# Group norm of the last RWKV chunk in two column ranges, its channel groups inside the projection's steps, and the inverse's updates on all four quarters of TensorE

## What is computed

```python
def _rwkv7_step(S, inp):
    r, w, k, v, a, b = inp
    sa = jnp.einsum('bhij,bhj->bhi', S, a)
    S = S * w[:, :, None, :] + sa[..., None] * b[:, :, None, :] + v[..., None] * k[:, :, None, :]
    return S, jnp.einsum('bhij,bhj->bhi', S, r)
...
    mu = o.mean(-1, keepdims=True)
    var = jnp.square(o - mu).mean(-1, keepdims=True)
    o = ((o - mu) * lax.rsqrt(var + LNX_EPS)).reshape(B, T, D) * lnx[0] + lnx[1]
    o = o + (jnp.sum(rh * kh * r_k, -1, keepdims=True) * vh).reshape(B, T, D)
    out = (o.astype(x.dtype) * g) @ w_out
```

## Time and profile before

| | us |
|---|---|
| median of 3 runs | 1201.16 |
| the profiled execution's own time | 1203.65 |
| its span, first to last instruction | 1201.9 |
| TensorE's granted clock over the span | 0.949 of full speed |
| from the end of the sixth chunk's levels to the projection's first matmul, by the trace | 47.5 |

### The profile page before, as it was taken

One profiled execution on the slowest core, in us unless ns is written; L12 is line 12 of the kernel. 1 busy time (PEld: TensorE's weight loads), 2 busy tenths in 40 slices (PEclk: granted clock), 3 DMA queues, 4 the chain that ended last, 5 costly groups with the idle time before them and its releaser, 6 DMA issues.

```text
span 1201.9 us, 23503 instructions
## 1 busy us (share of the span) xinstructions
PE 1075.0 (89%) x10193; PEld 755.6 (63%) x10194; DVE 537.5 (45%) x1052; ACT 358.0 (30%) x720; POOL 70.2 (6%) x101
## 2 busy tenths in 40 slices
PE   4989988899978969999999799998878599999994
PEld 3977987899955654445553499976646544444542
DVE  5856535656457561222122654485433731212215
ACT  3435524443322431111110534463232511111102
POOL 2002000011000000000000111021100000000000
PEclk8989979999987979999999999999988899999998
DMA  9503020011031939999999902454752489999992
GB/s 332 209 23 70 1 66 3 3 38 38 26 120 65 361 144 408 423 423 423 423 423 404 385 12 92 165 216 148 270 209 68 184 338 422 422 423 423 422 412 84
DMA packets 58251, 274.16 MB, mean 228 GB/s; under 512 B 5169, under 2 KB 5690, under 8 KB 34082
## 3 DMA queue, kind: packets, MB, share of 16 engines
q1 hardware_dynamic: 48160, 237.58, 49.2%
q0 software_dynamic: 9360, 34.72, 9.0%
q10 hardware_dynamic: 626, 0.32, 0.1%
HBM read 266.18 MB, written 6.46 MB: 227 GB/s over the span
## 4 chain that ended last, share of the span: by engine, by line
PE 75%; DVE 11%; DMA 6%; ACT 3%; issue 2%; DVEq 1%; SPq 0%; POOLq 0%; ACTq 0%; POOL 0%
PE ps L742 69%; DMA arena<-in_moe_w_up 5%; ACT arena L1492 2%; PE ps L883 1%; PE ps L1381 1%; DVE arena L1932 1%; DMA arena<-in_cache_k 1%; ACT arena L1495 1%; DVE arena L2195 1%; PE ps L1089 1%; PE ps L1206 1%; DVE pwr_lo L1938 0%; DMA arena<-in_x_prompt 0%; DVE arena L2032 0%; PE ps L1254 0%
## 5 line engine op out<-in xcount | busy, mean ns | idle before, releaser
L742 PE MATMUL ps<-arena 64*64 64x64 f32 (+10 forms) x7348 | 621.4, 321 | 51.7 <-DVE arena L2382 10.8
L742 PEld LDWEIGHTS ps<-arena 64*64 64x64 f32 (+4 forms) x7348 | 353.6, 140 | 295.7 <-issue 215.2
L1495 ACT COPY arena<-ps 128x512 f32<-128x512 f32 (+7 forms) x294 | 121.5, 433 | 330.8 <-PE ps L742 182.2
L2277 DVE TENSOR_TENSOR arena<-arena,ps 128x512 f32<-128x512 f32 x16 | 17.3, 1084 | 164.2 <-PE ps L742 164.2
L1492 ACT ACTIVATE arena<-ps,arena 128x256 f32<-128x256 f32 (+5 forms) x96 | 45.6, 508 | 125.1 <-PE ps L742 94.5
L2288 DVE SCALAR_TENSOR_TENSOR yy_lo<-ps,arena,yy_hi 128x512 fp32r<-128x512 f32 x32 | 22.7, 747 | 123.1 <-ACT yy_hi L1492 123.1
L1492 ACT ACTIVATE pw_hi<-arena 128x1024 fp32r<-128x1024 f32 x40 | 42.0, 1057 | 89.5 <-PE ps L742 83.1
L742 PE MATMUL ps<-px_hi,pw_hi 128*128 128x336 f32 x192 | 62.7, 326 | 3.1 <-DVE px_lo L2165 1.8
L742 PE MATMUL ps<-px_lo,pw_hi 128*128 128x336 f32 x192 | 60.9, 317 | 0.0
L742 PE MATMUL ps<-px_hi,pw_lo 128*128 128x336 f32 x192 | 60.7, 316 | 0.0
L1492 ACT ACTIVATE yy_hi<-ps,arena 128x512 fp32r<-128x512 f32 x32 | 20.5, 684 | 106.3 <-PE ps L742 106.3
(11 more groups left out here) (227 smaller groups left out, 1386.4 us busy)
## 6 DMA issues: line engine op xcount, KB each, us to landing
arena<-in_moe_w_gate SPq DMA_DIRECT2D x64, 1024.0 KB, 15.4
arena<-in_moe_w_up SPq DMA_DIRECT2D x64, 1024.0 KB, 18.6
arena<-in_moe_w_down SPq DMA_DIRECT2D x64, 1024.0 KB, 16.8
arena<-in_rwkv_w_rkv SPq DMA_DIRECT2D x6, 2048.0 KB, 19.4
arena<-in_w_kv_shared SPq DMA_DIRECT2D x4, 2048.0 KB, 19.7
arena<-in_cache_k POOLq DMA_DIRECT2D x16, 512.0 KB, 4.6
arena<-in_cache_v POOLq DMA_DIRECT2D x16, 512.0 KB, 6.6
arena<-in_rwkv_w_out SPq DMA_DIRECT2D x2, 2048.0 KB, 10.5
```

Source lines behind the costliest of these rows:

```text
L742: return pe.matmul(out, lhsT, rhs, start=start, stop=stop)
L1495: return act.copy(out, in_)
L2277: tt(HH.rearrange("p (k q) -> p q k", k=NF), HS.rearrange("p (q k) -> p q k", k=NF), bank(3).rearrange("p (q k) -> p q k", k=NF), ALU.mult ...
```

## The change

One matrix L is also written with its two heads exchanged, so that XI of a head lies on the other head's partitions; Y is made off the diagonal, the XI update on the diagonal and the XU update off it, into two banks that alternate. The last chunk's norm is split into columns 0 to 255 (earlier chunks, means before the last solution) and 256 to 335; variances go to 32 rows of each quarter of partitions, and so does the reciprocal; bonus sums and gates are pulled ahead and put into SBUF by ACT; the rest of each channel group's scaling follows inside the projection's steps. The state's output goes after the projection's sixth step. `w_out` is loaded by rows into slots 4 and 0.

```diff
+            return {5: 0, L_WO: 4, L_WO + 1: 0}.get(n, n % NSLOT)
...
+        def sums_bank(lv, hf):
+            return (0, 2)[(lv + 1) % 2] + hf
+        def products_bank(lv, hf):
+            return 2 * ((lv + hf) % 2)
...
-            sp.wait_ge(S("out_wkvp"), 32)
+            for h in range(2):
+                if h == 0:
+                    sp.wait_ge(S("wkvs_mm"), after("wkvs_mm", 8))
+                else:
+                    sp.wait_ge(S("st_mm"), NCH - 1)
...
+                        if layer == 0 and i == 2:
+                            sp.wait_ge(S("pw_lo"), 4)
+                        if layer == 0 and i == 3:
+                            sp.wait_ge(S("wkvp_mm"), after("wkvp_mm", 1))
...
+            pool.wait_ge(S("z_ready"), after("z_ready", 8))
+            gains(0, 0)
+            ld(mconst, cd[:, mconst0:mconst0 + nM], "in_mconst")
...
             pool.wait_ge(S("wkvp_ready"), after("wkvp_ready", 1))
             for hp in range(2):
                 pool.dma_start(O["new_wkv_prompt"][0, 0].rearrange("(c e) i j -> e i c j", e=2)[hp],
                                QW[:, :, 64 * hp:64 * hp + 64]).then_inc(S("out_wkvp"), 16)
...
                 for c in range(NC):
-                    for q in QH:
-                        m = mm(ps[q, 0, 64 * c:64 * c + 64], rav[q, c, 64:128], BK[q, c, 0:64])
+                    for hp, q in enumerate(QH):
+                        mm(ps[q, 0, 64 * c:64 * c + 64], rav[q, c, 64:128], BK[q, c, 0:64])
+                    for hp, q in enumerate(QH):
+                        m = mm(ps[QH[1 - hp], 2, 64 * c:64 * c + 64], rav[q, c, 64:128], BK[q, c, 0:64])
...
-                                m = mm(ps[q, hf, 64 * (c % 4):64 * (c % 4) + 64], LM[q, c, :], XU[k % 2][q, c, :])
+                                m = mm(ps[QH[1 - hp], sums_bank(lv, hf), 64 * (c % 4):64 * (c % 4) + 64], LM[q, c, :], XU[k % 2][q, c, :])
...
+                        b = products_bank(lv, hf)
+                        for c in range(4 * hf, 4 * hf + 4):
+                            cols = slice(64 * (c % 4), 64 * (c % 4) + 64)
+                            if lv < LEVELS[k] - 1:
                                 for q in QH:
+                                    mm(ps[q, b, cols], YI[q, c, :], XI[q, c, :])
+                            for hp, q in enumerate(QH):
+                                m = mm(ps[QH[1 - hp], b + 1, cols], XI[q, c, :], YI[q, c, :])
...
+            gate(0, 0, "g_mm")
+            gate(1, 2, "g_mm")
             right_sides(NCH - 1)
+            early_means(0, 1)
+            early_means(1, 3)
             solve(NCH - 1)
+            for i in range(2):
+                early_means(2 + i, 2 * i)
+            for i in range(2):
+                bonus(i, 1 + 2 * i, "bn_mm")
             outcome(NCH - 1)
+            for c in range(NC):
+                m = variances(c, slice(0, 256))
+            for j, b in enumerate((4, 7)):
+                for c in range(4):
+                    m = mm(ps[:, b, 80 * c:80 * c + 80], bones, T3[:, 4 * j + c, 256:T])
+            for i in range(2):
+                bonus(2 + i, 2 * i, "bt_mm")
+            for i in range(2):
+                bonus(4 + i, 1 + 2 * i, "bt_mm")
+            for c in range(NC):
+                m = variances(c, slice(256, T))
+            gate(2, 0, "gu_mm")
+            new_state(NCH - 1)
+            bonus(6, 2, "gu_mm")
+            for c in range(2):
+                deviations(c, 6 + c, "gr_mm")
+            bonus(7, 1, "gv_mm")
+            gate(3, 3, "gv_mm")
+            def norm_and_gate(k):
+                if k == 0:
+                    for c in (2, 3):
+                        pe.wait_ge(S("z_ready"), after("z_ready", c - 1))
+                        deviations(c, 4 + c, "gx_mm")
+                elif 0 < k < 5:
+                    c = k + 3
+                    pe.wait_ge(S("z_ready"), after("z_ready", 4 if c == 4 else c))
+                    deviations(c, 6, "gx_mm")
+                    gate(c, 7, "gx_mm")
+                elif k == 5:
+                    pe.wait_ge(S("z_ready"), after("z_ready", 8))
+                    for c in range(NC):
+                        m = mm(ps[0:64, 6 + c // 4, P * (c % 4):P * (c % 4) + P], ST[:, c, :], ident)
...
+                if l == 0 and t == 0:
+                    act.wait_ge(S("out_wkvp"), 32)
                 f(XTM[0][t][0:n, :].rearrange("t (k p) -> t p k", k=NC), YT[0:n, t, :].rearrange("t (p k) -> t p k", k=NC),
...
+            for c in range(2, NC):
+                wide_hi(0, 0, L_WO, c)
+                act.wait_ge(S("z_ready"), after("z_ready", c + 1))
+                px_hi(0, T3, c)
...
+                    if k == NCH - 1 and lv == 3:
+                        outcome(k - 1)
...
+                    if k == NCH - 1 and lv == 2:
+                        for c in range(NC):
+                            m = stt(rT[:, c, :], rT[:, c, :], rkv_[:, c:c + 1], kT_[:, c, :], ALU.mult, ALU.mult)
...
+            def gated(c):
+                bonus(c)
...
+                stt(sgT[:, c, :], sgT[:, c, :], lnx0[:, c:c + 1], bank(6 if c >= 4 else 6 + c % 2, T), ALU.mult, ALU.mult)
+                dve.drain()
+                stt(sgT[:, c, :], sgT[:, c, :], lnx1[:, c:c + 1], T2[:, c, :], ALU.add, ALU.add)
+                dve.drain()
...
+                tt(T3[:, c, :], sgT[:, c, :], x, ALU.mult).then_inc(S("z_ready"), 1)
...
+            gated(0)
+            state_sum(NCH - 1)
+            px_lo(0, T3, 0, 0)
+            dve.drain()
+            state_decay(NCH - 1)
+            gated(1)
+            px_lo(0, T3, 0, 1)
+            wide_lo(0, 0, L_WO, 1)
+            for c in range(2, NC):
+                gated(c)
+                wide_lo(0, 0, L_WO, c)
+                px_lo(0, T3, 0, c)
```

More of the change, by code:

```diff
@@ L668, in remainder @@
                                    ).then_inc(S(f"first_lo{l}"), 1)
+            pool.wait_ge(S("wkvp_ready"), after("wkvp_ready", 1))
+            for hp in range(2):
+                pool.dma_start(O["new_wkv_prompt"][0, 0].rearrange("(c e) i j -> e i c j", e=2)[hp],
+                               QW[:, :, 64 * hp:64 * hp + 64]).then_inc(S("out_wkvp"), 16)
             remainder(0)
@@ L1057, in out_proj @@
             def out_proj(place, m0, x0, aside):
-                for c in range(4):
-                    aside(c)
+                aside(-1)
                 for k in range(NC):
@@ L1074, in out_proj @@
                         m.then_inc(S("step_mm"), 1)
[L1075 to L1077 removed]
+                    aside(k)
             def rows_of(g):
@@ L1779, in px_hi @@
                 f(x_part(place, 0, c), X[:, c, :], ACT.Copy).then_inc(S("px_hi"), 1)
-            wide_hi(0, 0, L_WO, 0)
-            wide_hi(0, 0, L_WO, 1)
-            for c in range(NC):
+            act.wait_ge(S("ops_ready"), NCH)
+            f(DECS[:, 0, 0:1], eps_lnx, ACT.Sqrt)
+            for c in range(2):
+                act.wait_ge(S("g_mm"), after("g_mm", c + 1))
+                copy(T1[:, c, :], bank(2 * c, T)).then_inc(S("gate_ev"), 1)
+            wide_hi(0, 0, L_WO, 0)
+            solved(NCH - 1)
@@ new lines, in _ @@
+            act.wait_ge(S("bt_mm"), after("bt_mm", 1))
+            copy(rT[:, 2, :], bank(0, T)).then_inc(S("bt_ev"), 1)
+            act.wait_ge(S("vb_mm"), after("vb_mm", 1))
+            f(gnorm[:, 256:T], ps[:, 6, 256:T], ACT.Sqrt, scale=1.0 / N, bias=eps_lnx).then_inc(S("sd_b"), 1)
+            for i in range(3):
+                act.wait_ge(S("bt_mm"), after("bt_mm", i + 2))
+                copy(rT[:, 3 + i, :], bank((2, 1, 3)[i], T)).then_inc(S("bu_ev"), 1)
+            act.wait_ge(S("gu_mm"), after("gu_mm", 1))
@@ L1784, in _ @@
+            copy(T1[:, 2, :], bank(0, T)).then_inc(S("gu_ev"), 1)
+            act.wait_ge(S("gu_mm"), after("gu_mm", 2))
+            copy(rT[:, 6, :], bank(2, T)).then_inc(S("gu_ev"), 1)
+            for c in range(2):
                 act.wait_ge(S("z_ready"), after("z_ready", c + 1))
                 px_hi(0, T3, c)
-                if c == 3:
-                    wide_hi(0, 0, L_WO, 2)
-            for k in range(3, NC):
-                wide_hi(0, 0, L_WO, k)
+                if c == 0:
+                    act.wait_ge(S("gv_mm"), after("gv_mm", 1))
+                    copy(rT[:, 7, :], bank(1, T)).then_inc(S("gv_ev"), 1)
+                    act.wait_ge(S("gv_mm"), after("gv_mm", 2))
+                    copy(T1[:, 3, :], bank(3, T)).then_inc(S("gv_ev"), 1)
@@ new lines, in _ @@
+            right_sides(NCH - 1)
+            for i in range(4):
+                two = slice(2 * i, 2 * i + 2)
+                dve.wait_ge(S("ma_mm"), after("ma_mm", i + 1))
+                stt(sgT[:, two, 0:256], bank((1, 3, 0, 2)[i]).rearrange("p (c n) -> p c n", c=2), -1.0 / N,
+                    T3[:, two, 0:256], ALU.mult, ALU.add).then_inc(S("gn_a"), 1)
+            for c in range(2):
+                dve.wait_ge(S("bn_mm"), after("bn_mm", c + 1))
```

(10 more changed lines are left out.)

270 lines of the change are left out of this document (137 added, 133 removed).

## The result

The changed kernel takes 1184.56 us (median; 1182.83 to 1187.11), the kernel before, on the same chip, 1202.82: ratio 0.985, 95% interval 0.983 to 0.987, 18.3 us less. The forecast was 1168. The profiled execution has a span of 1181.0.

The account below looks back on a forecast made before the run. Bounds: TensorE in chunks and projection, serial waits in the tail, latency in the router, weight stream in the experts. -12.7 - 26.7 + 5.5 = -33.9 from 1203.65 gives 1169.8, median 1167.3, said 1168; range 1157 to 1186.

Parts of the forecast that it names:

- inverse: Chunk loop: XI and XU updates run on four 64x64 quarters at once, 1.15 us a level; 12.7 us less.
- tail: From the sixth chunk's updates to the first projection matmul: some 20.8 us against 47.5, 26.7 us less.
- projection: From the first projection matmul to the first finished tile: 40.4 us against 34.9, 5.5 us more.
- queues: DMA issue order on SP and POOL: w_out earlier, gains and constants ahead of the state's output; taken at nothing.
- No cold start is paid if TensorE stays busy, as its list says: Projection: TensorE pays no slow start at a lowered clock, given work without gaps; no size given.
- Fours run as two: Chunk loop: four quarters run as two, the inverse gains nothing and L costs 6.3 us: 1186; chance 0.10.
- The floor: Chunk loop: matmul starts at least 21 ns apart, so updates take 1.35 us instead of 1.15: 1172; chance 0.07.
- VectorE paces the projection: Projection: VectorE's loop takes 6.5 us instead of 5.0, five steps cost 6 us more: 1174; chance 0.11.
- The clock falls in the chunk loop: Chunk loop: TensorE's idle share lowers its clock; five chunks cost some 50 us instead of winning 12.7: 1230; chance 0.03.
- The normed copy waits: After the projection: ScalarE's normed copy waits for the state's output, 9.4 us late beside expert loads: 1177; chance 0.08.
- Nothing measurable: Whole kernel: the tail's waits only move, no measurable change; chance 0.02.

Follow-up runs that it names:

- copy_wait_later: Changed kernel, ScalarE waiting for the state's output before the third normed copy instead of the first, POOL before its remainder: 1183.2 us, ratio 0.983.
- router_early: Changed kernel with POOL issuing the router's three constants after the sixth gated input instead of the eighth: 1177.2 us, ratio 0.977.
- stream_behind_constants: Changed kernel with SP waiting for the router's constants before it issues the first expert load: 1175.7 us, ratio 0.978.
- w_out_later: Changed kernel with SP issuing the first half of the output weights after the sixth chunk's front: one run, span 1182.6 us.
- cold_start_filled: both_waits with the last gate's matmul repeated four times into an unread bank ahead of the projection: 1173.0 us, ratio 0.973.
- updates_in_pairs: Changed kernel issuing all XI updates before the XU updates, and the first copy of L before the second: 1191.6 us, ratio 0.989.
- both_waits: Changed kernel with the edits of router_early and copy_wait_later together: 1174.9 us, ratio 0.977.
- best_version: Changed kernel with early constants, filler matmuls, state turned last, its output copied elsewhere, third logits and POOL's remainder moved ahead: 1174.0 us, ratio 0.975.
- filled_and_last: cold_start_filled plus the last state turned after the projection's last step and ScalarE's copies of it and normed copies later: 1174.0 us, ratio 0.975.

## Why the prediction was right and where it was not

The direction and the mechanisms of the inverse and the tail held; the size was about twice what came. The median lies in the range, 1.4 us inside its upper end of 1186, and that is in part luck: the end was drawn for rivals that did not come, while a wait taken at nothing cost 7.7. By its steps, up to the first tile, in us:

| step | forecast | measured | how |
|---|---|---|---|
| inverse | -12.7 | -11.3 | chunk loop 165.4 to 154.1 |
| tail | -26.7 | -24.3 | 47.5 to 23.2 |
| projection | +5.5 | +9.2 | 34.9 to 44.1 (end of first tile) |
| queues | 0 | +7.7 | 382.2 to 389.9 |
| sum | -33.9 | -18.7 | medians: -18.3 |

Three of the forecast's numbers are not those of their own terms. The tail's list of 19.7 and an uncovered 1.5 make 21.2, not 20.8. The projection's terms make about 41.8, not 40.4: 34.9 less four gates (2.4) and a slow start of 1.7 (the first step took 7.03 us, the second 5.31), and 11.0 of new work and waits. The clock's fall in the chunk loop would decide at about 54% of the loop, not 40%, since by the forecast's own prices a full-clock loop wins 12.7 and a slow one costs 50, with 21.2 won elsewhere.

**Queues, the step that failed.** "Taken at nothing" was worked out for one waiter, ScalarE's normed copy, and that copy indeed costs nothing (copy_wait_later). The step named that POOL issues gains and constants ahead of the state's output, and that the expert stream follows the eighth gated input, late in the projection; it did not ask who waits for the constants, which follow the same input. VectorE does, for the router's constants, ahead of the first tile. The price it put on late company for the rival (a landing of 19.2 instead of 2.6) was the right kind of number on the wrong transfer. router_early and stream_behind_constants each take the 7.7 away.

**Inverse.** A level's 64 records take 1.16 us (forecast 1.15): four 64x64 quarters do run at once. The start distance of about 25 ns, for which the forecast cites the Trainium skill, "TensorE: Matmul & The Clock Gate", section "Wait — 56ns, not 53.3ns?", does not agree with this trace: 18 ns a record over the burst, and four starts within 58 ns. The second L is free: a front's 96 records take 2.08 us, about what 64 took. By chunk 2.0, 1.6, 2.9, 3.4, 0.9, 0.5 us were won of 0.9, 2.5, 2.8, 2.8, 2.5, 1.2 forecast. The fifth and sixth are short because of the gaps of 1.00 and 1.23 us that no wait explains; with the load moved (w_out_later) the fifth wins 2.8. The second is short because its clock sank further than before, 0.92 against 0.96 (the windows of the changed kernel and of the one before):

```profile
178.00:216.50 38.50, 32.58 (x977) 30.29 (x977) 25.50 (x50) 18.39 (x30) 0.00 (x0) 0.92 0.01 3
```

```profile
184.00:224.00 40.00, 35.01 (x944) 32.62 (x944) 25.55 (x49) 18.32 (x30) 0.00 (x0) 0.96 0.01 3
```

In stream_behind_constants, cold_start_filled and w_out_later its clock was 0.95 and it lasted 37.7 to 37.8 us; in the changed kernel and its other variants with four quarters at once 0.91 or 0.92 and 38.5 to 38.9. That the load of w_out moves under the chunk loop stood in the step on queues as "there earlier", at no cost.

**Tail.** 23.2 against 20.8 (21.2 by its terms), and alike in every variant. TensorE's list is 21.07 instead of 19.7; the eight late means were costed by columns at 1.1 and take 2.0: 16 records of 80 columns need 125 ns each, no less than the records of 128 columns. The bare end is 2.17 us, not 1.5: it holds the last of the three VectorE passes and 0.40 us ahead of it in which VectorE waits for nothing that the profile shows, px_hi, and two copies that stand behind px_hi in ScalarE's list.

**Projection.** 44.1 against 40.4. "No cold start is paid if TensorE stays busy, as its list says" failed, and the forecast had the idle time itself: 1.5 us bare at the tail's end, 2 us of waiting for the fourth gated input. The 2.17 us ahead of the projection and a wait of 1.17 us at 349.0 for the fourth gated input were each followed by some seven records at the lower level: the first step took 6.54 us instead of 5.09, the third 7.25 instead of 5.67, 3.0 us in all. For the first gap cold_start_filled shows that it was the cause; behind the second wait the clock fell in only five of eleven profiles. The later steps are 5.66 us, 5.3 forecast, since four short records of 336 columns take 1.5 us and not 1.2. VectorE does not pace them: past the third step no wait of TensorE is over 0.2 us.

**Rivals.** Fours run as two: fell (1.16 us, not 2.1). The floor: fell (18 ns a record, under its 21). VectorE paces the projection: no. The clock falls in the chunk loop: 1.00 from the third chunk on in the changed kernel; in the second it cost about 1 us. The normed copy waits: fell, though the landing it feared (12.1 us for the state's output) came; the wait for the constants ended later than its own would have. Nothing measurable: fell.

## What to carry to other kernels

When a change moves a wait, list every transfer issued behind it and every engine that waits for each, small ones first: 8 KB that one engine needs, issued at the same moment as a stream of megabytes, land when the stream lets them, here 12.7 instead of 2.8 us. Issue such loads early, or let the stream wait for them while the engines have slack later. And where work is moved to close gaps, look at the last few dependent passes: a gap of 2.17 us cost itself and, in seven of eight profiles, 1.4 to 1.6 us more in clock.

## What the runs showed of the hardware that was not expected

- Four 64x64 quarters take four records in 58 ns, the time that two records took on two.
- TensorE's idle "issue" time in the chunk loop went with data transfers: a gap of 1.00 us stood beside a 2 MB load and left when the load was moved, and one of 1.23 us grew to 2.87 where the load came. In the changed kernel TensorE's instruction loads are 7.4 us apart beside the 2 MB, 3.4 to 6.3 otherwise; in updates_in_pairs the same spacing brought no gap.
- Behind the same wait of 1.17 to 1.29 us the granted clock fell in five of eleven profiles of nearly the same list and stayed in six.
- VectorE instructions of 0.2 us stood 2.7 and 2.8 us beside a POOL subtraction of 2.86 us, in two kernels; those hit read and wrote SBUF alone. In the changed kernel (POOL 399.2 to 402.1), both_waits (391.7 to 394.6) and best_version (390.3 to 393.1) VectorE copied out of PSUM beside the same subtraction, and the copies kept their times: 0.49 for 128x320, as in filled_and_last, where they run alone. The Trainium skill, "SBUF — State Buffer", section "SBUF: two separate sides", speaks of a port pair that VectorE and GpSimd hold exclusively for a whole instruction; these rows agree for the instructions within SBUF.
